# Mixture-of-experts stage of a decoder block: blocks of four 32-slot units, experts in an order ranked on chip

## What is computed

```python
    gp = jax.nn.softmax(xf @ w_rg.astype(f32), axis=-1)
    gprob, gidx = lax.top_k(gp, 1)
...
    eprob, eidx = lax.top_k(jax.nn.softmax(el, axis=-1), TOP_K)
    eprob = eprob / jnp.sum(eprob, axis=-1, keepdims=True)
    gates = gprob * eprob
...
    def expert_block(args):
        xb, e = args
        hid = jax.nn.silu(xb @ w_gate[e]) * (xb @ w_up[e])
        return hid @ w_down[e]
...
    out = jnp.zeros((T, d), ys.dtype).at[buf_tok].add(ys * buf_w[:, None].astype(ys.dtype))
```

## Time and profile before

| | us |
|---|---|
| median of 3 runs | 2386.32 |
| lowest to highest | 2384.8 to 2388.15 |
| the profiled run | 2389.32 |
| its span | 2387.5 |
| PE busy (share of the span) | 2160.4 (90%) |
| DVE, ACT, POOL busy | 1216.1, 904.8, 475.9 |

### The profile page before, as it was taken

One profiled execution on the slowest core, in us unless ns is written; L12 is line 12 of the kernel. 1 busy time (PEld: TensorE's weight loads), 2 busy tenths in 40 slices (PEclk: granted clock), 3 DMA queues, 4 the chain that ended last, 5 costly groups with the idle time before them and its releaser, 6 DMA issues. The chain is left out here.

```text
span 2387.5 us, 33351 instructions
## 1 busy us (share of the span) xinstructions
PE 2160.4 (90%) x9900; PEld 1220.1 (51%) x9901; DVE 1216.1 (51%) x2408; ACT 904.8 (38%) x2111; POOL 475.9 (20%) x366
## 2 busy tenths in 40 slices
PE   5999999999999898897999998999939998999980
PEld 2666634444455446896777774555523333333320
DVE  4344356765345743555888776777642222222223
ACT  1333121111233311224779774434314434444434
POOL 0000033331111102344333110011121222222220
PEclk9999999999999998998999999999969999999995
DMA  8444113322356636885323324454546888888738
GB/s 345 151 150 159 66 65 112 141 89 88 102 184 231 195 128 191 267 272 201 98 85 107 103 93 157 162 149 153 202 160 207 268 276 315 279 280 300 205 76 299
DMA packets 182740, 424.45 MB, mean 178 GB/s; under 512 B 41513, under 2 KB 81321, under 8 KB 169721
## 3 DMA queue, kind: packets, MB, share of 16 engines
q1 hardware_dynamic: 159784, 352.33, 42.3%
q0 software_dynamic: 13472, 45.26, 8.1%
q10 hardware_dynamic: 9392, 25.74, 3.0%
HBM read 303.13 MB, written 124.85 MB: 179 GB/s over the span
## 5 line engine op out<-in xcount | busy, mean ns | idle before, releaser
L2352 PE MATMUL ps<-big,bias 128*64 x672 | 302.7, 604 | 2.9 <-DVE ex_wgu L2444 2.1
L2353 PE MATMUL ps<-ex_wgu,bias 128*64 128x512 f32 x672 | 302.7, 604 | 0.0
L345 PE MATMUL ps<-cp_wt,big 128*128 128x344 f32 x768 | 225.2, 453 | 0.0
L1870 PE MATMUL ps<-w_out,mo_yt 128*128 128x512 f32 x512 | 225.1, 597 | 0.0
L345 PEld LDWEIGHTS ps<-cp_wt,big 128*128 128x128 f32 x768 | 145.7, 191 | 76.8 <-issue 3.8
L1602 PE MATMUL ps<-at_v,at_pt 128*128 128x128 f32 (+1 forms) x1200 | 183.3, 291 | 0.5 <-DMA at_v<-v_d 0.5
L2352 PEld LDWEIGHTS ps<-big,bias 128*64 128x64 f32 x672 | 89.9, 139 | 182.2 <-issue 182.2
L1668 ACT ACTIVATE at_p<-at_p,at_low 128x256 f32<-128x256 f32 (+1 forms) x384 | 174.0, 456 | 19.1 <-DVE at_low L1631 18.8
L2403 ACT COPY ex_wgu<-big 128x4096 f32 x42 | 151.5, 3608 | 62.8 <-SPq L2273 31.8
L1602 PEld LDWEIGHTS ps<-at_v,at_pt 128*128 128x128 f32 x1200 | 149.5, 192 | 47.0 <-issue 36.4
L2364 PE MATMUL ps<-w_out,bias 128*64 x336 | 153.2, 598 | 2.6 <-DVE mod L2428 1.5
(11 more groups left out here) (349 smaller groups left out, 3716.1 us busy)
## 6 DMA issues: line engine op xcount, KB each, us to landing
big<-in_w_gate_up SPq DMA_DIRECT2D x32, 2048.0 KB, 11.2
w_out<-in_w_down SPq DMA_DIRECT2D x32, 1024.0 KB, 5.7
cp_w<-in_w_ada SPq DMA_DIRECT2D x24, 1024.0 KB, 5.2
ch_d<-pc_cv SPq DMA_DIRECT2D x20, 1024.0 KB, 4.3
at_v<-v_d SPq DMA_DIRECT2D x27, 512.0 KB, 3.9
o_d<-at_o SPq DMA_DIRECT2D x48, 264.0 KB, 2.1
mo<-o_d SPq DMA_DIRECT2D x16, 792.0 KB
pc_qkv<-ch_d SPq DMA_DIRECT2D x16, 768.0 KB, 5.4
```

The lines of the kernel that those rows point to most:

```text
L345: last = nc.tensor.matmul(ps[:, ROW_A + g, 0:THIRD], m.ht[:, k, t * P:(t + 1) * P], wt[:, k, g * THIRD:(g + 1) * THIRD], start=(k == 0), s ...
L1870: last = nc.tensor.matmul(ps[:, 2 + 2 * b + n, :], yt[:, b, k, :], w[:, k, n * BANK:(n + 1) * BANK], start=(k == 0), stop=(k == KD - 1))
L2352: nc.tensor.matmul(ps[0:HB, 2 + b, :], xt[:, b, k, 0:HB], wgu[:, bass.ds(at * WGU + k * 2 * DE, 2 * DE)], start=(k == 0), stop=(k == KD - 1))
L2353: last = nc.tensor.matmul(ps[HB:P, 2 + b, :], xt[:, b, k, HB:P], wgu2[:, b, k, :], start=(k == 0), stop=(k == KD - 1))
```

## The change

**Units.** `UN = 4` units of 32 slots make a block: PE's four column groups of 32 columns, each with its own expert's weights. `pad` is rounded with a shift of 5 instead of 6, the table of a block has four buffer numbers, and the lists are fetched by four instructions of POOL (one for each quarter) instead of two. An expert with a single unit that has another such expert within the three places before it gets a second, empty unit (`lone`, `near`), so that a block never spans more experts than there are buffers to hold. By the reference's routing the counts need 81 units of 64 (41 blocks, 42 with the one that makes the number even) and 143 units of 32; two are added by `near`, 145 in all, 37 blocks, 38 with the even one.

**Copies.** The first unit streams from the buffer, three others need copies. `wgu2` is now one block deep (3 x 128x4096) and copied in halves: half 0 (row chunks 0 to 3) of block t+1 once PE has passed the middle of gate_up(t) (`gu_half`), half 1 after gate_up(t). ACT copies unit 1, DVE units 2 and 3. The down copies go to free places in `mod`, `cst` and `bias`, one block deep, after down(t-1): ACT copies 128x2048 and two 128x1024, DVE one 128x2048. `xt`, `sg`, `hid` and `hidt` are one block deep instead of two. DVE's half 1 stands between the gated product and `take_idx`.

**Order of experts.** At tile 14 of 16 in `mix_and_route`, DVE ranks the experts of each group by their counts over the first 1280 tokens (`order_experts`) and makes an order in which large and small ones take turns; `m.order` holds it. Loads of experts 0 to 3 wait for `order_ready` and read the order.

**Loads.** SP no longer waits for arrivals; ACT and DVE wait for the loads themselves. For each expert SP issues gate-up of e and then down of e-1.

```diff
-HB = P // 2
-NBLK = (2 * T // HB + NE) // 2
+UN = 4
+HB = P // UN
+NBLK = (2 * T // HB + 2 * NE) // UN
...
+                sp.wait_ge(*order_ready.n(1))
+                first = [sp.value_load(m.order[0:1, e:e + 1], min_val=0, max_val=NE - 1) for e in range(NWB)]
...
-                for n in range(2):
+                for n in range(UN):
...
+                def order_experts():
+
+                    link(V.scalar_tensor_tensor(score[:, :], iota, 1.0 / NE - T, base[:, 0, :], ALU.mult, ALU.add))
...
+                    link(V.tensor_tensor(ranked, its_group, one_of, ALU.is_gt))
+                    link(V.tensor_reduce(place_of[:, :].rearrange("p (j g) -> p j g", g=NG), ranked, AX.X, ALU.add))
...
+                    link(V.tensor_tensor(chosen, along(place_of[:, :]), down_of(iota), ALU.is_equal))
+                    link(V.tensor_tensor(table, chosen, along(iota), ALU.mult))
+                    link(V.tensor_reduce(nth[:, 0:NE], table, AX.X, ALU.add))
+                    link(V.tensor_tensor(step[:, :], nth[:, 1:], nth[:, 0:NE], ALU.subtract))
+                    V.tensor_copy(m.order[:, :], nth[:, 0:NE]).then_inc(*order_ready.inc)
...
+                    if is_tile(t, NT - 2):
+                        order_experts()
...
+                link(V.tensor_tensor(chosen, chosen, along(pad[:, :]), ALU.mult))
+                link(V.tensor_reduce(pad[:, :], chosen, AX.X, ALU.add))
+                link(V.tensor_scalar(lone[:, 3:], pad[:, :], 1.0, None, ALU.is_le))
+                link(V.tensor_tensor(near[:, :], lone[:, 0:NE], lone[:, 1:NE + 1], ALU.add))
+                link(V.tensor_tensor(near[:, :], near[:, :], lone[:, 2:NE + 2], ALU.add))
+                link(V.scalar_tensor_tensor(near[:, :], near[:, :], 1.0, lone[:, 3:], ALU.min, ALU.mult))
+                link(V.tensor_tensor(pad[:, :], pad[:, :], near[:, :], ALU.add))
...
+                def load_next(e, b):
+
+                    last = free(e - 1)
+                    load_gate_up(e, b, free(e))
+                    load_down(e - 1, (b - 1) % NWB, last)
...
                     for k in range(KD):
-                        nc.tensor.matmul(ps[0:HB, 2 + b, :], xt[:, b, k, 0:HB], wgu[:, bass.ds(at * WGU + k * 2 * DE, 2 * DE)], start=(k == 0), stop=(k == KD - 1))
-                        last = nc.tensor.matmul(ps[HB:P, 2 + b, :], xt[:, b, k, HB:P], wgu2[:, b, k, :], start=(k == 0), stop=(k == KD - 1))
+                        if k % (KD // 2) == 0:
+                            pe.wait_ge(*gu_by_act.n(t * 2 + (1 + k // (KD // 2))))
+                            pe.wait_ge(*gu_by_dve.n(t * 2 + (1 + k // (KD // 2))))
+                        nc.tensor.matmul(ps[0:HB, 2 + b, :], xt[:, k, 0:HB], wgu[:, bass.ds(slot * WGU + k * 2 * DE, 2 * DE)], start=(k == 0), stop=(k == KD - 1))
+                        for u in range(1, UN):
+                            last = nc.tensor.matmul(ps[u * HB:(u + 1) * HB, 2 + b, :], xt[:, k, u * HB:(u + 1) * HB], wgu2[:, u - 1, k * 2 * DE:(k + 1) * 2 * DE], start=(k == 0), stop=(k == KD - 1))
...
                 for t, b, q, head, tail in blocks(act):
...
+                    if not tail:
+                        next_weights = weights_of(t + 1)
+                        copy_gate_up(t + 1, 0, next_weights)
                     act.wait_ge(*gu_done.n(t + 1))
...
                     if not tail:
                         take_x(t + 1, *after(b, q))
+                        copy_gate_up(t + 1, 1, next_weights)
...
+                    copy_down(t, weights)
...
                 for t, b, q, head, tail in blocks(dve):
...
+                    if not tail:
+                        next_weights = weights_of(t + 1)
+                        copy_gate_up(t + 1, 0, next_weights)
                     dve.wait_ge(*gu_done.n(t + 1))
...
                     if not tail:
+                        copy_gate_up(t + 1, 1, next_weights)
                         dve.wait_ge(xg_in[b], q * 16 + 16)
                         take_idx(t + 2, b)
                     if not head:
                         take_y(t - 1, *before(b, q))
+                    copy_down(t, weights)
```

More of the change, by code:

```diff
@@ L2269, in _ @@
             def _(sp):
-                def arrived(b, gu, down):
-                    sp.wait_ge(*wgu_in[b].n(gu))
-                    sp.sem_inc(*gu_loaded.inc)
-                    sp.wait_ge(*wd_in[b].n(down))
-                    sp.sem_inc(*d_loaded.inc)
-                def load_down(e, b):
-                    sp.dma_start(wd[:, b * WD:(b + 1) * WD].rearrange("p (k n) -> p k n", k=DE // P), one(a["w_down"], e)).then_inc(*wd_in[b].inc)
-                for b in range(NWB - 1):
-                    arrived(b, 0, 0)
@@ L2294, in _, with expert, free, load_gate_up @@
-                arrived(NWB - 1, NE // NWB - 1, NE // NWB - 1)
+                def expert(e):
+                    return sp.value_load(m.order[0:1, bass.ds(e, 1)], min_val=0, max_val=NE - 1)
+                def free(e):
+                    return sp.value_load(m.by_expert[0:1, bass.ds(e, 1)], min_val=0, max_val=NBLK)
+                def load_gate_up(e, b, blocks_done):
+                    sp.wait_ge(*gu_done.n(blocks_done))
+                    sp.sem_inc(seen_sp, 1)
+                    sp.dma_start(wgu[:, b * WGU:(b + 1) * WGU].rearrange("p (k n) -> p k n", k=KD), one(a["w_gate_up"], expert(e))).then_inc(*wgu_in[b].inc)
@@ L2296, in _ @@
+                with sp.Fori(0, NE // NWB - 2) as i:
+                    for b in range(NWB):
+                        load_next(NWB * i + (NWB + 1 + b), (b + 1) % NWB)
+                for e in range(NE - NWB + 1, NE):
+                    load_next(e, e % NWB)
+                load_down(NE - 1, NWB - 1, free(NE - 1))
             @block.gpsimd
@@ new lines, in take_x, with weights_of, copy_gate_up @@
+                    nc.scalar.copy(xt[:, :, :].rearrange("p k n -> p (k n)"), ps[:, 0:2, :].rearrange("p k n -> p (k n)")).then_inc(*xt_ready[b].inc)
+                def weights_of(t):
+                    return started(act, t), at(act, t, 1), at(act, t, 2)
+                def copy_gate_up(t, h, weights):
+                    half = WGU // 2
+                    if h:
+                        act.wait_ge(*gu_done.n(t))
+                    else:
+                        for b in range(NWB):
+                            act.wait_ge(*wgu_in[b].n(loads_of(b, weights[0])))
+                        act.wait_ge(*gu_half.n(t))
+                    nc.scalar.copy(wgu2[:, 0, h * half:(h + 1) * half], wgu[:, bass.ds(weights[1] * WGU + h * half, half)]).then_inc(*gu_by_act.inc)
@@ new lines, in copy_down @@
+                def copy_down(t, weights):
+                    for b in range(NWB):
+                        act.wait_ge(*wd_in[b].n(loads_of(b, weights[0])))
+                    act.wait_ge(*y_done.n(t))
+                    nc.scalar.copy(m.mod[:, 2 * D:4 * D], wd[:, bass.ds(weights[1] * WD, WD)])
+                    for k in range(DE // P):
+                        ins = nc.scalar.copy(wd2[1][k], wd[:, bass.ds(weights[2] * WD + k * D, D)])
+                    ins.then_inc(*d_by_act.inc)
@@ new lines, in copy_gate_up @@
+                def copy_gate_up(t, h, weights):
+                    half = WGU // 2
+                    if h:
+                        dve.wait_ge(*gu_done.n(t))
+                    else:
+                        for b in range(NWB):
+                            dve.wait_ge(*wgu_in[b].n(loads_of(b, weights[0])))
+                        dve.wait_ge(*gu_half.n(t))
+                    for u in (2, 3):
+                        ins = nc.vector.tensor_copy(wgu2[:, u - 1, h * half:(h + 1) * half], wgu[:, bass.ds(weights[u - 1] * WGU + h * half, half)])
+                    ins.then_inc(*gu_by_dve.inc)
```

222 lines of the change are left out of this document (124 added, 98 removed).

## The result

| | before | after |
|---|---|---|
| median time, four runs each | 2386.55 us | 2355.53 us (2352.19 to 2360.17) |
| ratio | | 0.9874 (95%: 0.9859 to 0.989) |
| profiled execution, its span | 2389.3, 2387.5 us | 2352.3, 2350.5 us |
| first silu | 1800.7 | 1804.4 |
| first to last silu | 512.5, 42 blocks | 464.5, 38 blocks |

The kernel became 31 us faster; 27 were forecast. The two profiled executions are 37.0 us apart: +3.7 before the phase, **-48.0** in it, **+7.3** behind it.

The account below looks back on a forecast made before the run. PE was taken to bound the experts phase, 11.99 us a block and never idle in the block traced; -30.9 us in the phase and +4.1 at the routing's end made -26.8 on 2386.3, so 2360 us, range 2332 to 2398.

Parts of the forecast that it names:

- Fewer blocks, four together: Experts phase on PE: 38 blocks for 42, four column groups running together at 11.99 us a block, -48.0 us.
- C: Rival on PE: issue limits four groups, +0.96 us a block, 2373, or 2397 at 63 ns a record; chance 0.10.
- D: Rival on PE: pairs of column groups run one after the other, 22.3 us a block, about 2710; chance 0.04.
- Copies on ACT: ACT in each block: 9.4 us of work fits by little before the next gate_up ends; price 0.
- E: Rival on ACT: register table reads are not hidden, 15 us a block, 2433 in all; chance 0.06.
- The late gather: DVE copies delay the index copy, gather issued 2.5 us later, slack 7.4 us: 1.0 us of stall a block, 31 us.
- Density: DMA engines in the experts phase: 95% busy at 12.0 us a block, 88% at 13.0, taken as consistent with 1.0 us stall.
- Weight stalls: Weight loads in the experts phase: buffers free two or more blocks early save one, so the old 11 us go.
- Turns of the loop: PE at loop turns in the experts phase: 19 turns at 0.35 us, 7 us, as before.
- Routing's end: Before the experts phase: list rows ready 5.2 us later, fetch +1.6, four fetches for two +2.5, together +4.1 us.
- Sum: Experts phase 481.6 us for 512.5, -30.9; with +4.1 at the end of routing, -26.8 in total.
- Rival A: Experts phase: stalls all but vanish, 0.2 us a block, gain 55.8 less 4.1, 2334; chance 0.10.

Follow-up runs that it names:

- indices-first kernel: Changed kernel with DVE's wait for gathered rows and its index copy moved to the block's start: 2336.0 us (0.9795 of before), again 2339.7 us (0.9792).
- experiment 6: Changed kernel with the natural order of experts and the loads issued as before, leaving four column groups alone: 2434.3 us, 1.0194 of before.
- the repeat: The changed kernel run once more without any edit, on one chip beside two of its variants: 2353.3 us, 0.9851 of before.
- no empty block: Changed kernel without the last, empty block, so 37 blocks and one loop pair less: 2339.7 us, 0.9818 of before.

## Why the prediction was right, point by point

The time was forecast at 2360 and is 2355.5. The core of it held: PE needs for a block what it needed before, and gathers that are issued late are the main loss. But two terms were wrong in opposite directions, and that the total came so close is in part luck.

- *Fewer blocks, four together:* 11.97 us a block for 11.99, passes 0.43 us apart. Right, -48.0. C and D are out. That the phase is shorter by 48.0 in sum as well is chance: the stalls were 20.9 us before and are 21.6 after, of other kinds. The column-group figures of the Trainium skill ("TensorE: Matmul & The Clock Gate", Part 3) pointed the right way; the case I built on its 62 ns for each matmul (Part 2), that loads cost as much, is excluded: four loads and four matmuls pass here in 427 ns, 53 ns a record.
- *Copies on ACT:* "fits by little" is exact: half 0 ends 0.76 or 0.00 us before silu. Table reads are hidden (E is out).
- *The late gather:* the mechanism is right and proved by moving one copy. Issue was forecast 4.5 us after the start and is 4.0 or 4.8 to 5.7. **The step that failed is its size**: I took the excess of the four slowest of 16 landings and got 1.0 us a block, 31 in all. In the same stretch of the new kernel no gather is as slow as those four: of those issued 4.8 us and later most land in 4 to 7, of those issued at 4.0 most take 8 to 10, hardly above the slack, so many turnings wait a little. It is 17.6 us before PE's matmuls for the 31 forecast, and 14.8 on the clock, 0.5 a block.
- *Density:* DMA engines 95% busy at 12.0 us a block were read as a sign that 12.0 would not hold. The indices-first kernel runs 12.1 at 0.97 (2010 to 2200). A high share told when landings grow, not that anyone waits.
- *Weight stalls:* PE had none, as forecast (DVE waited for weights in three places, 9.5 us in all). But "so the 11 us go" priced the order by what it removes from before. What it and the loads prevent in the new kernel is 79 us (experiment 6). "No arrival stands before another issue" was stated and given no price; it is 11.
- *Turns of the loop:* 7 forecast. In the changed kernel 2.8 show, as waits for gathers cover the rest; all that is left in the indices-first phase is 448.4 - 37 x 11.97 = 5.5 us.
- *Routing's end:* PE's transposes of the lists at 1777.8 for 1773.6, +4.2 for +4.1, by the steps named: rows ready at 1770.63, fetch at 1771.63, four fetches. The ranking costs nothing that shows.
- *The phase's end:* **left out, and +7.3.** The prediction gave no term to the last block, where no gate_up covers ACT's copies. From last silu to result copy it is 6.4 us more: 1.4 at the exit of the loop, 3.2 for the bare copies, 1.7 for the lower clock. It wanders, too: 84.0 us from the last silu to the end in the repeat for 81.6 here.
- *Sum:* the phase came out 17.1 us better than forecast, the tail 7.3 worse, the start 0.4 better: 37.0 for 26.8 in the profiled executions. The medians differ by 31.0, because this execution of the changed kernel was among its quickest and before's among its slowest.
- Rival A (stalls all but vanish, 2334) did not come, but is just what the indices-first kernel gives: 2336 and 2340.

## What to carry to other kernels

When copies are added to an engine, ask which small instruction behind them releases a transfer, and put that one first: a 0.15 us copy of indices cost 15 us here. A change that packs more work into a block shortens the lead of every load, so its order and its queue are part of it and must be priced in the new kernel, not by the stalls of the old. Walk through the last block by itself: whatever was hidden behind the next block is bare there.

## What the runs showed beyond that

- **Leaving the loop seems to cost by the passes skipped.** The loop has 23 pairs of blocks under an `If`. PE stood on "issue" at its exit 1.1 us with 3 pairs skipped (before), 2.52 with 5 (after), 3.7 with 6 (no empty block): some 0.4 to 0.6 us each. No run varies the number of skipped pairs alone, so this reading of three points isn't shown. The Trainium skill ("Advanced Engine Details and Errata", Control Flow Timing) gives about 0.11 us for a compare and branch; by this reading a skipped pair costs several times that.
- **POOL's descriptors slow beside DVE's copies.** Issue of a gather takes 0.97 us in the changed kernel; with the indices first about half of the gathers fall under the half-0 copies and take up to 2.4, the others 0.97 again. The Trainium skill ("SBUF — State Buffer", "SBUF: two separate sides") describes that DVE's copy holds the port with which POOL writes descriptors; the trace agrees in direction, and behind the early issue no cost of it shows.
- **The clock after a gap on PE.** After 2.31 us of waiting in the phase (above), and after 4.74 us without work in the tail, the clock fell; behind the latter it was 0.66 over the 5 us from 2280, that is, the lower level (1.2 GHz) for a part of them, with records of 1.06 us for 0.59. In the repeat of the changed kernel it fell after the 2.52 us at the loop's exit as well, in the first profile not.
- **The unchanged part wanders.** In thirteen profiles of the changed kernel and its variants, alike up to there but for an instruction or two, the first silu stood anywhere from 1800.9 to 1811.2 us. Two single profiles can't be compared in their totals to better than that; stage by stage they can.
